# Means of squares and norms of the attention outputs moved from VectorE to GpSimd, two operations per half head

## The reference

```python
fox_o = forgetting_attention(fq, fk, fv, log_f)               # 8 heads of 64
fox_o = rms_norm(fox_o, fox_out_norm)                          # per head and token
gdn_o = gated_delta_chunked(cq, ck, cv, g, beta)               # 4 heads of 128
gate  = silu(gz)
gdn_o = rms_norm(gdn_o, gdn_out_norm) * gate
mixed = concatenate([fox_o, gdn_o], axis=-1) @ w_out
x = x + rms_norm(mixed, post_mix_norm)                         # then the MLP with its own norms
```

## Time and profile before

| | us |
|---|---|
| median of 3 runs | 1513.58 |
| lowest, highest | 1505.16, 1516.79 |
| the profiled execution's own time | 1514.45 |
| its span in the trace | 1512.7 |
| from 340 to 700 us: TensorE busy, GpSimd busy, VectorE busy | 322.5, 203.6, 229.2 |
| from 700 to 766 us: TensorE busy, GpSimd busy, VectorE busy | 49.1, 34.0, 33.0 |

### The profile page before, as it was taken

One profiled execution on the slowest core, in us unless ns is written; L12 is line 12 of the kernel. 1 busy time (PEld: TensorE's weight loads), 2 busy tenths in 40 slices (PEclk: granted clock), 3 DMA queues, 4 the chain that ended last, 5 costly groups with the idle time before them and its releaser, 6 DMA issues.

```text
span 1512.7 us, 20659 instructions
## 1 busy us (share of the span) xinstructions
PE 1405.4 (93%) x7389; PEld 1187.4 (78%) x7389; DVE 966.2 (64%) x1506; ACT 650.2 (43%) x1342; POOL 668.3 (44%) x582
## 2 busy tenths in 40 slices
PE   6899999978989899898799979999999999999997
PEld 4688888857878889797678868887888778888885
DVE  6777777746566665765434598766666675444557
ACT  6554334434454454554523352333333244445453
POOL 3633333217465483663610256666666354443001
PEclk9999999998999999999689989999999999999999
DMA  6133333254132031010322224444444896333533
GB/s 203 42 113 111 112 112 111 84 181 140 29 98 57 30 112 43 15 43 24 103 84 84 84 84 144 144 148 145 150 147 149 283 346 210 98 98 98 208 96 142
DMA packets 135324, 177.87 MB, mean 118 GB/s; under 512 B 10492, under 2 KB 82732, under 8 KB 135224
## 3 DMA queue, kind: packets, MB, share of 16 engines
q1 hardware_dynamic: 135224, 176.56, 36.5%
HBM read 124.05 MB, written 52.48 MB: 117 GB/s over the span
## 4 chain that ended last, share of the span: by engine, by line
PE 58%; POOL 14%; DVE 11%; DMA 7%; issue 6%; ACT 2%; SPq 2%; POOLq 0%; DVEq 0%; ACTq 0%
PE ps L2632 6%; PE ps L2573 6%; PE ps L2575 6%; PE ps L2574 6%; PE ps L2891 6%; PE ps L2893 6%; PE ps L2892 6%; DMA w_bot<-in_w_up_dram 5%; PE ps L2757 3%; PE ps L2830 2%; PE ps L2832 2%; PE ps L2831 2%; PE ps L2637 2%; POOL s_act L2474 2%; POOL s_act L2475 2%
## 5 line engine op out<-in xcount | busy, mean ns | idle before, releaser
L2891 PE MATMUL ps<-db_hi,da_hi 128*128 128x512 f32 x448 | 175.5, 392 | 4.4 <-DVE db_lo L2182 4.3
L2893 PE MATMUL ps<-db_hi,da_lo 128*128 128x512 f32 x448 | 174.4, 389 | 0.0
L2892 PE MATMUL ps<-db_lo,da_hi 128*128 128x512 f32 x448 | 174.4, 389 | 0.0
L2180 DVE TENSOR_TENSOR da_lo<-a_raw,da_hi 128x512 fp32r<-128x512 f32 x112 | 85.8, 766 | 122.5 <-ACT da_hi L1666 122.4
L1666 ACT ACTIVATE da_hi<-a_raw 128x512 fp32r<-128x512 f32 x112 | 70.7, 631 | 159.7 <-PE ps L2893 135.8
L2878 PE MATMUL ps<-bt_hi,ring_hi 128*128 128x512 f32 x320 | 127.8, 399 | 4.9 <-DVE ring_lo L2102 3.6
L2880 PE MATMUL ps<-bt_hi,ring_lo 128*128 128x512 f32 x320 | 126.5, 395 | 0.0
L2879 PE MATMUL ps<-bt_lo,ring_hi 128*128 128x512 f32 x320 | 125.6, 393 | 0.0
L2573 PE MATMUL ps<-i_bt_hi,i_ring_hi 128*128 128x512 f32 x280 | 111.3, 397 | 3.2 <-DVE i_u L1855 3.2
L2575 PE MATMUL ps<-i_bt_hi,i_ring_lo 128*128 128x512 f32 x280 | 110.7, 396 | 0.0
L2574 PE MATMUL ps<-i_bt_lo,i_ring_hi 128*128 128x512 f32 x280 | 110.5, 395 | 0.0
(11 more groups left out here) (351 smaller groups left out, 3757.7 us busy)
## 6 DMA issues: line engine op xcount, KB each, us to landing
a_raw<-act_dram SPq DMA_DIRECT2D x112, 256.0 KB, 2.6
act_dram<-s_act SPq DMA_DIRECT2D x64, 256.0 KB, 2.0
wd<-in_w_down_dram SPq DMA_DIRECT2D x15, 1024.0 KB, 7.7
act_dram<-c SPq DMA_DIRECT2D x48, 256.0 KB, 5.0
w_top<-in_w_up_dram SPq DMA_DIRECT2D x18, 512.0 KB, 4.6
w_bot<-in_w_up_dram SPq DMA_DIRECT2D x16, 512.0 KB, 5.7
i_top<-in_w_in_dram SPq DMA_DIRECT2D x14, 512.0 KB, 4.0
i_bot<-in_w_in_dram SPq DMA_DIRECT2D x14, 512.0 KB, 5.3
```

What stands on the lines that cost most here:

```text
L2891: nc.tensor.matmul(acc, da_hi[s][:, cols], db_hi[s][:, :], start=start, stop=False, skip_group_check=True)
L2892: nc.tensor.matmul(acc, da_hi[s][:, cols], db_lo[s][:, :], start=False, stop=False, skip_group_check=True)
L2893: return nc.tensor.matmul(acc, da_lo[s][:, cols], db_hi[s][:, :], start=False, stop=stop, skip_group_check=True)
```

## The change

The means and the norms of all tails go from VectorE to GpSimd. The squared row sums of the fox heads go to ScalarE, as one activation of 128x4 with the function Square and the constant in its scale. The means stay in front of the powers, now on the same engine. The norm of a half head is two operations of GpSimd instead of four of VectorE: one multiplies four tiles at a time (128x4x64 or 128x4x128) with the powers, broadcast along the row, and one with the weight row or the gate. The second waits for the first. In the plan a norm stands once, at the time where the first of VectorE's four stood. `mixed_ready` counts one per half head. TensorE's and SP's lists keep their order; what SP waits for at L1043 is now the norm on GpSimd.

```diff
--- before.py
+++ after.py
@@ -176,10 +176,9 @@
             at("pool", t + 1.0, "z", h)
         if c % 4 == 3:
             tail = ("gdn", h, c // 4)
-            at("dve", t + 4.0, "tail_mean", tail)
+            at("pool", t + 4.0, "tail_mean", tail)
             at("pool", t + 4.1, "tail_power", tail)
-            for k in range(4):
-                at("dve", t + (6.0 + 0.4 * k if last else 8.0 + 2.0 * k), "tail_norm", "gdn", (h, c - 3 + k))
+            at("pool", t + (6.0 if last else 8.0), "tail_norm", "gdn", (h, c // 4))
 
 
 def fox_weight(i):
@@ -228,10 +227,10 @@
             at("sp", b, "load", "fox", n + 1)
         if qb % HT == HT - 1:
             tail = ("fox", n, qb // HT)
-            at("dve", v + 1.9, "tail_mean", tail)
+            at("pool", v + 1.9, "tail_mean", tail)
             at("pool", v + 2.0, "tail_power", tail)
-            for k in range(HT):
-                at("dve", v + (3.6 + 0.3 * k if i == NFT - 1 else 5.0 + 1.5 * k), "tail_norm", "fox", (n, qb - HT + 1 + k))
+            at("act", v + 0.8, "rr", tail)
+            at("pool", v + (3.6 if i == NFT - 1 else 5.0), "tail_norm", "fox", (n, qb // HT))
 
 
 for _p in range(GDN_HEADS):
@@ -253,16 +252,16 @@
 POOL_PREP = numbered_of("pool", "power", "decay", "kd", "kbg", "qd", "level", "R0")
 TAILS = [item[1] for item in ORDER["pool"] if item[0] == "tail_power"]
 TAIL = numbered(TAILS)
-MEAN = numbered([item[1] for item in ORDER["dve"] if item[0] == "tail_mean"])
+MEAN = numbered([item[1] for item in ORDER["pool"] if item[0] == "tail_mean"])
 NORM_SUM = numbered_of("dve", "mean")
-FOX_RR = numbered([tail for tail in MEAN if tail[0] == "fox"])
-NORMS = [item[1:] for item in ORDER["dve"] if item[0] == "tail_norm"]
+FOX_RR = numbered([item[1] for item in ORDER["act"] if item[0] == "rr"])
+NORMS = [item[1:] for item in ORDER["pool"] if item[0] == "tail_norm"]
 NORM = numbered(NORMS)
 
 
 def norms_of(t):
 
-    return max(count for (_, (_, tile)), count in NORM.items() if tile == t)
+    return max(count for (_, (_, half)), count in NORM.items() if half == t // HT)
 
 
 
@@ -1040,7 +1040,7 @@
             def load_w_out(c):
                 if c >= 1:
                     sp.wait_ge(scan_done, (GDN_HEADS - 1) * NCHUNK)
-                    sp.wait_ge(mixed_ready, NORM[("gdn", (GDN_HEADS - 2, NT - 1))])
+                    sp.wait_ge(mixed_ready, NORM[("gdn", (GDN_HEADS - 2, 1))])
                 if c >= 7:
                     sp.wait_ge(w_out_lo, c - 6)
                 sp.dma_start(w_out_raw[c % 7][:, :, :], w_out_k[:, :, c * P:(c + 1) * P]).then_inc(group_loaded[NT + c], 16)
@@ -1465,6 +1465,16 @@
                 if i >= 1:
                     act.wait_ge(fox_read, i)
                 nc.scalar.activation(sq_fox[:, :], fox_o[:, 0:FOX_DIM], ACT.Square, accum_out=fox_ss[:, hh, qb:qb + 1]).then_inc(fox_read, 1)
+
+
+            def row_sum_squares(tail):
+
+                _, n, half = tail
+                cols = slice(half * HT, (half + 1) * HT)
+                act.wait_ge(fox_exp, n * NT + (half + 1) * HT)
+                if n >= 2:
+                    act.wait_ge(tail_mean, MEAN[("fox", n - 2, half)])
+                nc.scalar.activation(fox_rr[:, n % 2, cols], row_sum[:, n % 2, cols], ACT.Square, scale=(FOX_DIM * EPS) ** 0.5).then_inc(rr_ready, 1)
 
             def o_out(h, c):
 
...
@@ -1989,38 +2001,6 @@
                     dve.wait_ge(state_ready, h * (NCHUNK + 1))
                 nc.vector.memset(state[:, :], 0.0).then_inc(state_ready, 1)
 
-
-            def mean(tail):
-
-                what, n, half = tail
-                cols = slice(half * HT, (half + 1) * HT)
-                if what == "gdn":
-                    dve.wait_ge(gdn_square_done, n * NCHUNK + (half + 1) * HT)
-                    nc.vector.tensor_scalar(gdn_ms[:, cols], gdn_ss[:, cols], GDN_DIM * EPS, None, ALU.add).then_inc(tail_mean, 1)
-                    return
-                r, rr = row_sum[:, n % 2, cols], fox_rr[:, n % 2, cols]
-                dve.wait_ge(fox_read, n * NT + (half + 1) * HT)
-                nc.vector.scalar_tensor_tensor(out=rr, in0=r, scalar=FOX_DIM * EPS, in1=r, op0=ALU.mult, op1=ALU.mult).then_inc(rr_ready, 1)
-                dve.wait_ge(rr_ready, FOX_RR[tail])
-                nc.vector.tensor_tensor(fox_ms[:, n % 2, cols], fox_ss[:, n % 2, cols], rr, ALU.add).then_inc(tail_mean, 1)
-
-            def fox_norm(n, qb):
-
-                h, hh = divmod(n, 2)
-                dve.wait_ge(tail_power, TAIL[("fox", n, qb // HT)])
-                dve.wait_ge(masks_ready, 4)
-                o = mixed_fox(qb // HT, h)[:, qb % HT, hh * FOX_DIM:(hh + 1) * FOX_DIM]
-                nc.vector.scalar_tensor_tensor(out=o, in0=o, scalar=fox_ms[:, n % 2, qb:qb + 1], in1=fox_norm_row[:, :],
-                                               op0=ALU.mult, op1=ALU.mult).then_inc(mixed_ready, 1)
-
-            def gdn_norm(h, c):
-
-                dve.wait_ge(tail_power, TAIL[("gdn", h, c // HT)])
-                dve.wait_ge(z_normed, h + 1)
-                o = mixed_gdn(c // HT, h)[:, c % HT, :]
-                nc.vector.scalar_tensor_tensor(out=o, in0=o, scalar=gdn_ms[:, c:c + 1], in1=z_tok[h % 2][:, c, :],
-                                               op0=ALU.mult, op1=ALU.mult).then_inc(mixed_ready, 1)
-
             for item in ORDER["dve"]:
                 kind, n = item[:2]
                 if kind == "mean":
@@ -2404,8 +2378,38 @@
                 pool.wait_ge(masks_ready, 4)
                 nc.gpsimd.tensor_tensor(z_tok[h % 2][:, :, :], z_tok[h % 2][:, :, :], stacked(gdn_norm_row[:, :], NT), ALU.mult).then_inc(z_normed, 1)
 
+
+            def mean(tail):
+
+                what, n, half = tail
+                cols = slice(half * HT, (half + 1) * HT)
+                if what == "gdn":
+                    pool.wait_ge(gdn_square_done, n * NCHUNK + (half + 1) * HT)
+                    nc.gpsimd.tensor_scalar(gdn_ms[:, cols], gdn_ss[:, cols], GDN_DIM * EPS, None, ALU.add).then_inc(tail_mean, 1)
+                    return
+                pool.wait_ge(rr_ready, FOX_RR[tail])
+                pool.wait_ge(fox_read, n * NT + (half + 1) * HT)
+                nc.gpsimd.tensor_tensor(fox_ms[:, n % 2, cols], fox_ss[:, n % 2, cols], fox_rr[:, n % 2, cols], ALU.add).then_inc(tail_mean, 1)
+
+            def norm(what, n, half):
+
+                done = NORM[(what, (n, half))]
+                cols = slice(half * HT, (half + 1) * HT)
+                pool.wait_ge(tail_power, TAIL[(what, n, half)])
+                pool.wait_ge(masks_ready, 4)
+                if what == "fox":
+                    h, hh = divmod(n, 2)
+                    o = mixed_fox(half, h)[:, :, hh * FOX_DIM:(hh + 1) * FOX_DIM]
+                    power, weight = wide(fox_ms[:, n % 2, cols], FOX_DIM), stacked(fox_norm_row[:, :], HT)
+                else:
+                    pool.wait_ge(z_normed, n + 1)
+                    o, power, weight = mixed_gdn(half, n), wide(gdn_ms[:, cols], P), z_tok[n % 2][:, cols, :]
+                nc.gpsimd.tensor_tensor(o, o, power, ALU.mult).then_inc(mixed_scaled, 1)
+                pool.wait_ge(mixed_scaled, done)
+                nc.gpsimd.tensor_tensor(o, o, weight, ALU.mult).then_inc(mixed_ready, 1)
+
             for item in ORDER["pool"]:
-                kind, n = item
+                kind, n = item[:2]
                 if kind == "power":
                     norm_power(n)
                 elif kind == "decay":
```

More of the change, by code:

```diff
@@ L597, in build @@
         z_normed = sem("z_normed")
+        mixed_scaled = sem("mixed_scaled")
         mixed_ready = sem("mixed_ready")
@@ L1436, in read @@
                 if what == "z" and g == 0 and p >= 2:
-                    act.wait_ge(mixed_ready, NORM[("gdn", (p - 2, NT - 1))])
+                    act.wait_ge(mixed_ready, NORM[("gdn", (p - 2, 1))])
                 if what == "fv" and g == 0 and p >= 2:
@@ L1515, in _ @@
                     k_hi(n)
+                elif kind == "rr":
+                    row_sum_squares(n)
                 else:
@@ L2043, in _ @@
                     scan_v_new(n, item[2])
-                elif kind == "state":
+                else:
                     scan_state(n, item[2])
-                elif kind == "tail_mean":
-                    mean(n)
-                elif n == "fox":
-                    fox_norm(*item[2])
-                else:
-                    gdn_norm(*item[2])
             heads_over(dve)
@@ L2428, in _ @@
                     power(n)
+                elif kind == "w_out":
+                    w_lo_part(n)
+                elif kind == "tail_mean":
+                    mean(n)
                 else:
-                    w_lo_part(n)
+                    norm(n, *item[2])
             heads_over(pool)
```

## The result

| | median us | lowest to highest | executions |
|---|---|---|---|
| before | 1513.03 | 1505.16 to 1516.79 | 14 |
| after | 1520.44 | 1517.22 to 1524.39 | 14 |

The change costs 7.4 us: the ratio is 1.0058, with a 95% interval of 1.0044 to 1.0071. The forecast was 1511, 2 us under the time before; its range of 1494 to 1525 holds the result. The profiled execution of the changed kernel took 1522.22 us, with a span of 1520.4.

What follows compares the result with a forecast made beforehand. TensorE, busy 93% of the span, was taken as the bound, with VectorE's norms and `fox_rr` in its chain of waits. From 1514.45 us, -11.2 - 2.1 + 9.6 = -3.7 gave 1511 us, range 1494 to 1525.

Steps and rivals of the forecast that it cites:

- 11.2 on the chain: VectorE's tail operations leave TensorE's chain of waits at 500 to 560, 560 to 620 and 700 to 766: 11.2 us gained.
- 2.1 on w_out: w_out's loads go out before GpSimd's first `big_lo` there, and ScalarE's wait at 718.2 goes: 2.1 us gained.
- Five places have no cover: Tails at about 454, 613, 721, 735 and the last delay TensorE or the end, 9.6 us together; other tails cost nothing.
- I give the clock nothing, because waits go and others come: Over the whole kernel, no change of time from TensorE's clock was counted in the sum: 0 us.
- 1.4 + 3.4: Last stretch: a fox norm before queries at about 721 costs 1.40 us, a gdn norm before queries at about 735 costs 3.4.
- About 454: A fox norm comes behind `z_tok` and in front of queries for which TensorE already waits 2.3 us: 1.40 us cost.
- the last tail: At 763.5 ScalarE's wait of 2.42 us for the last tail gets 0.4 us longer.
- At 613: Two norms and two means stand before `decay` and the new head's k powers: 3.0 us cost, with a wait for k's norm.
- the two signs of being wrong: Fast side: the last stretch's half level falls from 30 to under 15 us; slow side: `q_lo` or `n_lev` waits over 20.
- GpSimd becomes the engine that TensorE waits for: Rival: tails before the queries in most half heads expose half of GpSimd's added 47 us: +19 us, 1533; chance 0.15.
- Hidden anyway: Rival: gains and costs at the tails both land in waits that others set: within 2 us of 1514; chance 0.25.
- The cover holds, and the clock comes back: Rival: only 454, 721 and the end cost, and the last 66 us lose their half level: 1489 us; chance 0.15.

Runs made afterwards that it cites:

- the last reordered kernel: The changed kernel with every norm behind the next pair of queries, except one behind head 3's first power and one behind the 44th tile's queries: 1498.83 us, ratio 0.9911.
- four sets of places: Norms in the changed kernel's places, 1520.44 us; behind masks, 1511.32; behind the next pair of queries, 1506.00; the same with two moved once more, 1498.83.
- the one such place that was tried: The kernel before, norms still in VectorE but moved behind the attention's next row maximum, at most two behind one: 1523.24 us, ratio 1.0073.

## Why the prediction was wrong

**Right.** Each operation on GpSimd: fox passes 0.616 + 0.730 = 1.35 us against 1.40, gdn passes 1.043 + 1.274 = 2.32 against 2.36, a mean 0.23 against 0.25; in all 43 us of busy time against 47. For VectorE 57 less was said and 44 came. The relief, 11.2 on the chain and 2.1 on w_out, stands against 15 measured with the norms left out; but that size is in part luck. Between the kernel before and the one without norms TensorE's idle time falls by 8.0 us on the pages (107.3 to 99.3) and its busy time by 9.8 (1405.4 to 1395.6), and the prediction had only waits. The w_out loads are out before the first `big_lo`, ScalarE's wait for them is gone, and TensorE's for the exponential behind it. The means cost nothing (ratio 1.000). The rule of the Trainium skill (GPSIMD Engine Reference, Engine selection) that two-input work is about twice as slow on GpSimd would have given 1520, the time that came; but the trace does not bear out its way there. The passes together take 1.35 and 2.32 us where VectorE's four operations took 1.82 and 2.33. That is with their waiting: half of VectorE's took no more than 0.279 and 0.346 us, four of which make 1.12 and 1.38.

**The step that failed** is "Most tails meet time in which GpSimd waits anyhow. ... Five places have no cover", 9.6 us. It measured 23. In waits for `q_lo` alone the change added 15.5 us, 12.5 of them by the norms. Three things were wrong in it.
- It took GpSimd's idle time in front of `n_lev` as a sum over the stage and set the norms against it. What counts is whether there is idle time between the norm and the next item that TensorE waits for. At 475.7 to 482.4 there is none, and `n_lev` is no gap but more work ahead of the queries. That place was missing, 2.43 us, and another wait of 1.5 at 678.
- It priced the queries as if they had slack wherever TensorE had not waited so far. The plan puts each pair only 3.0 in front of its scores (`at("pool", b - 3.0, "queries", i)`), so what stands in front of it in GpSimd's list delays TensorE soon. Moving the norms behind the queries, and two of them away from a power, took 22 of the 23 us away at the same load. The code has a second limit, two buffers, each free when the tile two before is scored (`pool.wait_ge(fox_scored, i - 1)`); but in the trace GpSimd waits for that only once, 2.5 us, and at 481.91 the buffer had been free since about 467.7. Whether the queries could stand earlier in the list was not tried.
- Each place was priced by its wait alone. With the norms TensorE is idle 16.1 us longer and busy 9.4 us longer, at 25 us more of the half level. The relief has such a share too, 9.8 us, so in the sum of both it cancels, and TensorE's busy time is the same before and after. "I give the clock nothing, because waits go and others come" was near enough for the whole and wrong for each of its two terms.

At single places the prices were near for the last stretch as a sum (1.4 + 3.4 against 2.7 more at 731.5 and 4.75 at 745.4), and too small there by 2.7. About 454 and in the last tail they were small and stayed so: 2.72 us for the queries in place of 2.33, and 2.90 in place of 2.42. At 613 the price of 3.0 was right in size, but was paid elsewhere: the wait for k's norm did not come (9.4 us before and after), while the queries at 623.4 were waited for 3.49 us. The wait for the state fell to 6.3 and not under 5. The last stretch's half level went from 30 to (1 - 0.83) x 2 x 66 = 22 us, not under 15; of the two signs of being wrong, the one on the slow side came.

**The rivals.** "GpSimd becomes the engine that TensorE waits for", with the queries as the place, was the right mechanism, and its own point of decision, waits for `q_lo` over 19 us, was passed at 20.9. It had 0.15. Its price was too high (1533), because it took half of all the new GpSimd time for exposed, 24 us, where waits for `q_lo` grew by 15.5. Its evidence against, "only 5 of 63 tiles have waited so far", was weak: it tells of waits, not of how little slack the other 58 had. "Hidden anyway" falls with the kernel without norms. "The cover holds, and the clock comes back" at 1489 had a time near what the last reordered kernel reached (ratio 0.9911), but not by its mechanism: the half level of the last 66 us did not go there either, with a clock of 0.82. The gain was there all the same, and the place in the list decided whether it came.

## What to carry to other kernels

Work that is moved to an engine with idle time costs by what stands behind it in that engine's order, not by its length: the same 24 norms cost 23, 14, 8 or 1 us at four sets of places. So in a fixed list look for the items that the bottleneck reads soon after they are made, and try movable work right behind them and not in front; a total of idle time over a stage says nothing about that. On VectorE the one such place that was tried was worse than the old one, so measure each. And expect a new wait of TensorE to bring more than itself: here 16.1 us more of idle time went together with 9.4 more of busy time.

## What the runs showed of the hardware

- A small split is not cheaper on VectorE on the mean: `q_hi` 0.427 and `q_lo` 0.565 us for 128x128, against 0.420 and 0.469 on GpSimd in the last reordered kernel. Most single ones are shorter, and a few much longer; of VectorE's 64 `q_lo` (two inputs in SBUF, shortest, median and longest in ns), 2.45 us is about the length of GpSimd's operations of 128x1024, as in the earlier trace rows:

```profile
L2014 DVE TENSOR_TENSOR q_lo<-q,q_hi x64: 291/293/2450, 341.0 to 739.5; 128x128 fp32r<-128x128 f32 x64
```

- VectorE's gdn norms took 0.583 us on the mean before and 0.726 behind the maxima, with the same shape. The median did not move (0.346 and 0.348 us); the mean is raised by a few long ones, as at 618.46, where one takes 2.41 us beside GpSimd's `decay` of 2.34 us, which starts at 618.38. So what GpSimd does beside such an operation sets its length:

```profile
L2038 DVE SCALAR_TENSOR_TENSOR mixed_half<-mixed_half,gdn_ms,z_tok 128x128 f32<-128x128 f32 x32 | 22.6, 726 | 1.1 <-POOL gdn_ms L2409 1.1
```
